# Encoder layer with two attention branches: first modulation chunk on VectorE, rotary angles split, first cosine products on VectorE

## The reference

```python
mod = silu(c) @ w_ada + b_ada;  shift, scale, gate = split(mod, 3)
h = rms_norm(x, norm_pre) * (1 + scale) + shift
proj = h @ w_in          # qa ka va za qd kd vd zd gm, 11264 columns
qa, ka, qd, kd = rope(..., positions)   # [x1*cos - x2*sin, x2*cos + x1*sin]
ya = merge(dilated windows of qa, ka, va) * silu(za);  pa = ya @ w_proj_a
yd = rms_norm(differential_attention(qd, kd, vd)) * silu(zd);  pb = yd @ w_proj_b
ga, gb = split(sigmoid(gm));  y = (ga * pa + gb * pb) @ w_out
out = x + gate * rms_norm(y, norm_post)
```

## Time and profile before

| | |
|---|---|
| median of 3 runs | 847.47 us (846.45 to 848.08) |
| the profiled execution | 846.08 us |
| its span | 844.2 us |
| TensorE busy (PE) | 798.7 us, 95% of the span |
| VectorE (DVE), ScalarE (ACT), GpSimd (POOL) | 54%, 43%, 55% |
| granted clock of TensorE, mean | 0.983 |
| the chain that ended last | PE 71%, DVE 13%, issue 7%, ACT 4%, DMA 2% |

### The profile page before, as it was taken

The page is one execution under the profiler, slowest core; times in us unless marked ns, Lnnn a source line. Parts: engine busy times, 40 slices in busy tenths (PEclk is TensorE's granted clock), DMA queues, the critical chain, the costliest instruction groups (busy, mean ns, idle before and its releaser), DMA issues.

```text
span 844.2 us, 12690 instructions
## 1 busy us (share of the span) xinstructions
PE 798.7 (95%) x4614; PEld 672.0 (80%) x4614; DVE 454.4 (54%) x708; ACT 359.9 (43%) x777; POOL 466.4 (55%) x620
## 2 busy tenths in 40 slices
PE   5887999998999999999989998998999999999997
PEld 5666898886788888889768778877877778888897
DVE  3765363656736354334597588579657653103532
ACT  4543644443335444423435444454466442323310
POOL 4455642555627566377476486679357367647200
PEclk9999899999899999999999999999999999999999
DMA  9933323257333434144522243143112113324431
GB/s 318 326 124 99 101 76 114 76 172 244 97 113 88 136 91 126 50 126 121 147 75 76 82 120 102 51 139 101 50 51 75 51 53 122 101 75 135 165 100 50
DMA packets 87075, 95.38 MB, mean 113 GB/s; under 512 B 9405, under 2 KB 78310, under 8 KB 87014
## 3 DMA queue, kind: packets, MB, share of 16 engines
q1 hardware_dynamic: 86944, 94.56, 36.4%
q10 hardware_dynamic: 70, 0.02, 0.0%
HBM read 78.53 MB, written 5.54 MB: 100 GB/s over the span
## 4 chain that ended last, share of the span: by engine, by line
PE 71%; DVE 13%; issue 7%; ACT 4%; DMA 2%; SPq 1%; POOL 1%; DVEq 0%; POOLq 0%; ACTq 0%
PE proj L1695 49%; PE proj L1829 4%; PE sums L1620 3%; PE score L1570 3%; PE turned L1588 2%; PE proj L1753 2%; DVE dstat L1319 2%; PE score L1536 2%; ACT probs L1025 2%; PE sums L1622 2%; DVE dstat L1335 1%; DVE at_lo L1342 1%; DVE q_lo L1275 1%; PE score L1558 1%; ACT junk L1057 1%
## 5 line engine op out<-in xcount | busy, mean ns | idle before, releaser
L779 POOL TENSOR_TENSOR w_lo<-raw,w_hi 128x256 fp32r<-128x256 f32 x376 | 297.5, 822 | 212.9 <-ACT w_hi L901 212.8
L1695 PE MATMUL proj<-h_hi,w_hi 128*128 128x512 f32 x560 | 230.1, 411 | 0.0
L1695 PE MATMUL proj<-h_hi,w_lo 128*128 128x512 f32 x560 | 220.4, 394 | 0.0
L1695 PE MATMUL proj<-h_lo,w_hi 128*128 128x512 f32 x560 | 218.9, 391 | 0.0
L1695 PEld LDWEIGHTS proj<-h_hi,w_hi 128*128 128x128 f32 x560 | 105.7, 189 | 29.8 <-issue 8.9
L1695 PEld LDWEIGHTS proj<-h_hi,w_lo 128*128 128x128 f32 x560 | 105.5, 188 | 23.7
L1695 PEld LDWEIGHTS proj<-h_lo,w_hi 128*128 128x128 f32 x560 | 106.1, 189 | 19.7 <-issue 0.5
L901 ACT ACTIVATE w_hi<-raw 128x1024 fp32r<-128x1024 f32 x96 | 100.2, 1053 | 11.8 <-PE proj L1695 7.8
L809 POOL TENSOR_TENSOR rope_x<-rope_x,cos_t 128x512 f32<-128x512 f32 x36 | 56.7, 1574 | 75.4 <-DMA rope_s<-rope_x 75.4
L1342 DVE TENSOR_TENSOR at_lo<-turned,at_hi 128x512 fp32r<-128x512 f32 x64 | 44.0, 688 | 61.3 <-ACT at_hi L1043 60.7
L1025 ACT ACTIVATE probs<-score,dstat 128x512 f32<-128x512 f32 x64 | 43.4, 684 | 59.3 <-DVE dstat L1319 59.3
(11 more groups left out here) (286 smaller groups left out, 1563.0 us busy)
## 6 DMA issues: line engine op xcount, KB each, us to landing
raw<-in_w_in SPq DMA_DIRECT2D x85, 512.0 KB, 3.6
rope_s<-rope_x SPq DMA_DIRECT2D x144, 64.0 KB, 2.3
ada<-in_w_ada SPq DMA_DIRECT2D x24, 256.0 KB, 7.1
zd<-in_w_ada SPq DMA_DIRECT2D x8, 512.0 KB, 6.3
raw<-in_w_proj_b SPq DMA_DIRECT2D x8, 512.0 KB, 3.4
raw<-in_w_out SPq DMA_DIRECT2D x8, 512.0 KB, 4.2
rows_in<-window_rows SPq DMA_DIRECT2D x4, 792.0 KB, 4.8
window_rows<-rows_out SPq DMA_DIRECT2D x4, 528.0 KB, 3.7
```

Of the source, the lines that this page charges most:

```text
L779: nc.gpsimd.tensor_tensor(lo[:, k, :], raw_place(n)[:, k, :], hi.bitcast(F32)[:, k, :], ALU.subtract).then_inc(w_lo_done, 1)
L1695: ins = mm(dst, left, right, start=k == 0 and n == 0, stop=k == nk - 1 and n == 2, skip_group_check=tile.b == 2)
```

## The change

Five things are changed.
- VectorE sums all eight pieces of chunk 0; `ada_piece` and its three groups of eight matmuls are gone. The two copies of turned x stand behind piece 5.
- The angle work is cut in two: four instructions (position to the number of turns) ahead of modulate(0), seven (`angle_rest`) behind the last sum of chunk 2, with one sum of chunk 3 behind them, and then modulate(2).
- The sums of a chunk begin ahead of the modulate of the chunk before (one sum), and three instead of one stand ahead of the first h_rest.
- ScalarE's three Sin stand behind `cut_hi` of half 4 instead of behind half 2; SP stores the tables behind the last piece of chunk 3 and half 5.
- The cosine products of the first four tiles are made by VectorE from the PSUM banks into a tensor of their own (`first_cos_x`), ahead of tick 8. GpSimd no longer makes them. TensorE's `bank_free` waits for them too. In all ticks VectorE evacuates the v banks of stage 0 ahead of the rotary work instead of behind it.

```diff
--- before.py
+++ after.py
@@ -178,9 +178,7 @@
     mix_turn_at = by_tick(range(NT), lambda tt: free_turn(mix_tick[tt] + 4))
     vt_at = by_tick([t for t in tiles if t.kind == "vt"], lambda t: free_turn(t.last + (1 if t.j else 2)))
     G_TICK = 36
-    N_CH, PE_ADA = 4, (2, 5, 7)
-    DVE_ADA = [[kk for kk in range(KT) if ch or kk not in PE_ADA] for ch in range(N_CH)]
-    ADA_SUMS = [sum(len(p) for p in DVE_ADA[:ch + 1]) for ch in range(N_CH)]
+    N_CH = 4
     gate_row_at = by_tick(range(2), lambda i: G_TICK + KT + 1 + i)
     ya_split_tick = T0[10] + 4
     LAST_TICK = max(END, max(s.pv for s in steps) + 5)
@@ -342,6 +340,10 @@
         first_raw = sb("first_raw", [P, RAW, 4, BW], on=second)
         h_f = sb("h_f", [P, 2, S], on=second)
         second.close()
+        third = ExitStack()
+        sb("ahead_of_at", [P, 2, D], on=third)
+        first_cos_x = sb("first_cos_x", [P, 4, S], on=third)
+        third.close()
 
 
         def stage_tensors(parity, on):
@@ -455,6 +457,7 @@
         angle_done = sem("angle_done")
         lam_dots = sem("lam_dots")
         silu_done = sem("silu_done")
+        first_cos_done = sem("first_cos_done")
         xt_dve = sem("xt_dve")
         x_norm_done = sem("x_norm_done")
         ab_done = sem("ab_done")
@@ -580,6 +583,11 @@
             n = rope_no[tile.u]
             return (zd[:, n, :], zd[:, 4 + n, :]) if n < 4 else (rope_x2[:, n % 2, :], rope_s2[:, n % 2, :])
 
+        def cos_place(tile):
+
+            n = rope_no[tile.u]
+            return first_cos_x[:, n, :] if n < 4 else rope_place(tile)[0]
+
         def swapped_wait(engine, tile):
             n = rope_no[tile.u]
             if n < 4:
@@ -632,16 +640,16 @@
             sp.wait_ge(x_turned, KT)
             for kk in range(4):
                 load_ada(3, kk)
+            for kk in range(4, KT):
+                load_ada(3, kk)
+            load_half(5)
             sp.wait_ge(act_sin, 3)
             sp.dma_start(trig_rows.rearrange("q f a n -> (q f) a n"), trig).then_inc(trig_stored, 16)
-            for kk in range(4, KT):
-                load_ada(3, kk)
             sp.wait_ge(trig_stored, 16)
             for i in range(4):
                 for table, a in ((cos_t, 2), (sin_t, i % 2)):
                     sp.dma_start(table[32 * i:32 * i + 32, :].rearrange("f (q n) -> f q n", q=NT),
                                  trig_rows[:, :, a, :].rearrange("q f n -> f q n")).then_inc(trig_loaded, 16)
-            load_half(5)
             for i, v in enumerate((lambda_q1, lambda_k1, lambda_q2, lambda_k2)):
                 sp.dma_start(lam_in[:, i, :], v[0].partition_broadcast(P)).then_inc(small_loaded, 16)
 
@@ -801,10 +809,8 @@
             for half in prep_at(-1)[6:]:
                 cut_lo(half)
             for t in range(8, LAST_TICK + 1):
-                for tile in tiles[2 * (t - 8):2 * (t - 7)] if t < 10 else rope_at(t) if t >= 12 else []:
+                for tile in rope_at(t) if t >= 12 else []:
                     swapped_wait(pool, tile)
-                    if rope_no[tile.u] == 0:
-                        pool.wait_ge(trig_loaded, 128)
                     at = rope_place(tile)[0]
                     nc.gpsimd.tensor_tensor(at, at, cos_t[:], ALU.mult).then_inc(rope_cos_done, 1)
                 for half in prep_at(t):
@@ -940,16 +946,16 @@
             h_round(1)
             h_full(1)
             cut_hi(halves[2])
+            for k in (2, 3):
+                h_round(k)
+                h_full(k)
+            cut_hi(halves[3])
+            cut_hi(halves[4])
             act.wait_ge(angle_done, 1)
             for a, sign in enumerate((-1.0, 1.0)):
                 nc.scalar.activation(trig[:, a, :], angle, ACT.Sin, scale=sign).then_inc(act_sin, 1)
             act.wait_ge(angle_done, 2)
             nc.scalar.activation(trig[:, 2, :], complement, ACT.Sin).then_inc(act_sin, 1)
-            for k in (2, 3):
-                h_round(k)
-                h_full(k)
-            cut_hi(halves[3])
-            cut_hi(halves[4])
             for k in (4, 5):
                 h_round(k)
                 h_full(k)
@@ -1156,16 +1162,17 @@
                 dve.wait_ge(ada_loaded[ch][kk], 16)
                 kept = ada[ch][:, 0, :, :]
                 total = turned[:].rearrange("p (r n) -> p r n", r=2) if ch else kept
-                n = DVE_ADA[ch].index(kk)
-                if n == 0:
+                if kk == 0:
                     if ch == 0:
                         dve.wait_ge(silu_done, 1)
                     elif ch == 1:
                         dve.wait_ge(xt_act, 3)
+                    else:
+                        dve.wait_ge(ada_used, KT * ch)
                     ins = ts_(total, kept, silu_c[:, 1, 0:1], None, ALU.mult)
                 else:
-                    dve.wait_ge(ada_used, ADA_SUMS[ch] - len(DVE_ADA[ch]) + n)
-                    ins = stt(out=kept if kk == DVE_ADA[ch][-1] else total, in0=ada[ch][:, kk, :, :],
+                    dve.wait_ge(ada_used, KT * ch + kk)
+                    ins = stt(out=kept if kk == KT - 1 else total, in0=ada[ch][:, kk, :, :],
                               scalar=silu_c[:, 1, kk:kk + 1], in1=total, op0=ALU.mult, op1=ALU.add)
                 ins.then_inc(ada_used, 1)
 
@@ -1191,6 +1198,9 @@
                 link(ts_(angle, angle, rope_c[:, 0:1], None, ALU.mult))
                 link(ts_(turns, angle, float(1 / (2 * np.pi)), ROUND, ALU.mult, ALU.add))
                 link(ts_(turns, turns, ROUND, None, ALU.subtract))
+
+            def angle_rest():
+
                 for part in TWO_PI:
                     link(stt(out=angle, in0=turns, scalar=-part, in1=angle, op0=ALU.mult, op1=ALU.add))
                 ts_(angle, angle, PI_BELOW, -PI_BELOW, ALU.min, ALU.max).then_inc(angle_done, 1)
@@ -1198,32 +1208,37 @@
                 link(stt(out=complement, in0=angle, scalar=-1.0, in1=angle, op0=ALU.mult, op1=ALU.max))
                 ts_(complement, complement, -1.0, float(np.pi / 2), ALU.mult, ALU.add).then_inc(angle_done, 1)
 
-            for kk in DVE_ADA[0][:-1]:
+            for kk in range(6):
                 sum_ada(0, kk)
             for k in (4, 5):
                 dve.wait_ge(x_turned, k + 1)
                 nc.vector.tensor_copy(xt[:, k, :], turn_place(k)).then_inc(xt_dve, 1)
-            sum_ada(0, DVE_ADA[0][-1])
+            sum_ada(0, 6)
+            sum_ada(0, 7)
             dve.wait_ge(cols_done, 2)
+            angles()
             modulate(0)
-            angles()
-            sum_ada(1, 0)
+            for kk in range(3):
+                sum_ada(1, kk)
             h_rest(0)
-            sum_ada(1, 1)
+            sum_ada(1, 3)
             h_rest(1)
-            for kk in range(2, KT):
+            for kk in range(4, KT):
                 sum_ada(1, kk)
+            sum_ada(2, 0)
             modulate(1)
-            for kk in range(KT):
+            for kk in range(1, KT):
                 sum_ada(2, kk)
+            angle_rest()
+            sum_ada(3, 0)
             modulate(2)
-            sum_ada(3, 0)
             sum_ada(3, 1)
+            sum_ada(3, 2)
             h_rest(4)
-            sum_ada(3, 2)
             sum_ada(3, 3)
+            sum_ada(3, 4)
             h_rest(5)
-            for kk in range(4, KT):
+            for kk in range(5, KT):
                 sum_ada(3, kk)
             modulate(3)
             h_rest(6)
@@ -1248,6 +1263,15 @@
                 link(tt_(lam[:, 4:5], lam[:, 2:3], lam[:, 3:4], ALU.subtract))
                 link(ts_(lam[:, 5:6], lam[:, 4:5], LAMBDA_INIT, -1.0, ALU.add, ALU.mult))
                 link(ts_(cols[:, 41:42], cols[:, 40:41], 1.0 - LAMBDA_INIT, None, ALU.mult))
+
+            def first_cos(tile):
+                n = rope_no[tile.u]
+                dve.wait_ge(proj_done, tile.u + 1)
+                dve.wait_ge(rope_copied, n + 1)
+                if n == 0:
+                    dve.wait_ge(trig_loaded, 128)
+                stt(out=cos_place(tile), in0=proj[:, tile.u % 4, :], scalar=SCALE if tile.kind == "q" else 1.0, in1=cos_t[:],
+                    op0=ALU.mult, op1=ALU.mult).then_inc(first_cos_done, 1)
 
             def rope_turn(tile):
                 n = rope_no[tile.u]
@@ -1261,11 +1285,14 @@
                 n = rope_no[tile.u]
                 at, other = rope_place(tile)
                 dve.wait_ge(rope_sin_done, n + 1)
-                dve.wait_ge(rope_cos_done, n + 1)
+                if n < 4:
+                    dve.wait_ge(first_cos_done, n + 1)
+                else:
+                    dve.wait_ge(rope_cos_done, n - 3)
                 if n:
                     dve.wait_ge(rope_lo_done, n)
                 for dst, view in in_order(rope_o[:], tile):
-                    ins = tt_(dst, view(at), view(other), ALU.add)
+                    ins = tt_(dst, view(cos_place(tile)), view(other), ALU.add)
                 ins.then_inc(rope_done, 1)
 
             def rope_cut(tile):
@@ -1420,6 +1447,9 @@
```

(40 more changed lines are left out.)

## The result

| | before | after |
|---|---|---|
| median, measured together, 4 runs each | 847.78 us (846.45 to 851.1) | 838.46 us (837.12 to 838.84) |
| ratio of the two, 95% interval | | 0.9885 (0.9865 to 0.9904) |
| the profiled execution | 846.08 us | 837.12 us |
| its span | 844.2 us | 835.3 us |
| granted clock, mean | 0.983 | 0.979 |

A forecast was written before the change was run, and what follows sets the result against it. TensorE, nearly always busy, was taken to set the pace behind the first attention steps, so gains ahead reach the end. Terms -4.6, -4.4, -3.6, +2.9 gave -9.7: 836.4, or 837.8 us on the median's scale; range 832 to 844.5.

The forecast's parts named there:

- The sum: Whole kernel: opening -4.6, rotary -4.4, clock -3.6, new wait +2.9, in all 9.7 us earlier.
- Chunk 0: Opening: VectorE's sums replace three TensorE groups, first modulate near 19.5 instead of 23.76; gain there 4.2 us.
- Chunks 1 to 3: Opening: modulation(3) at 52.2 instead of 56.77, 4.6 us gained (bounds 3.6 and 5.5); seven angle instructions taken as 5.0 us.
- SP's queue: Tables' store takes 3.7 us (bounds 2 and 8.4); half 6 issued at 54.7, landed at 58.3; slack 0.8 us.
- The rival by SP's queue: Slow store and loads land half 6 at 68, eating the rotary gain; up to 853.5 us; slower had chance 0.07.
- First cosine products and v: Rotary part: VectorE's products cost nothing, last v at 74.5, first scores at 75.5, 9.0 us earlier; TensorE idles 1.2 us.
- The clock: Behind the first scores the upper level stays: scores 1.6 us instead of 3.2, 24 products 5.7 instead of 7.69; -3.6.
- The new wait: Ahead of TensorE's second transpose: 2.9 us, as GpSimd's cuts and the swap of tile 8 come only 7.0 us earlier.
- Where the step failed: Behind the second transpose: TensorE busy without break, nothing found that gives back time from the 9.7 us gained.
- given back: Rival: TensorE drops to the lower clock in the new wait, up to 3.5 us lost, 841.5 to 844.5; chance 0.20.
- a fall of the clock behind 76: Sign of being wrong: the granted clock falls behind 76 us, where 1.00 was forecast behind the first scores.
- More gained: Rival: the shifted 3.4 us wait up to 208.3 isn't followed by the slow clock; up to 4.5 us more, 833; chance 0.13.

The follow-up runs named there:

- c0_after: The changed kernel run and profiled again, with nothing altered: 838.77 us, 0.9894 of before.
- e8: The changed kernel with pieces 2, 5 and 7 of chunk 0 given back to TensorE: 840.47 us, 0.991 of before.
- e10: The changed kernel with the seven angle instructions ahead of modulate(1) and SP's swaps ahead of the loads of halves in every tick: 825.5 us, 0.9752 of before.
- e11: The kernel before with SP's swaps ahead of the loads of halves in every tick, nothing else: 842.57 us, 0.9942 of before.
- e9: The kernel before with only chunk 0 changed, VectorE summing all eight pieces: 841.76 us, 0.993 of before.
- e1: The changed kernel with the rotary part as before (cosine products by GpSimd, v behind the rotary work), so the opening alone: 841.74 us, 0.9939 of before.
- e5: The changed kernel with SP issuing the swap of tile 8 ahead of the loads of halves it stood behind: 833.15 us, 0.9832 of before.
- e2: The kernel before with only the rotary part changed (first cosine products by VectorE, v evacuated ahead): 845.65 us, 0.9979 of before.

## Why the prediction was right, point by point

The sum had -9.7 on the profile's scale and the profiles gave -9.0; the median came out 0.7 us above 837.8. The mechanism held up to the second transpose. The terms were off by more than the sum, and that their deviations cancelled in part was luck.

- **Chunk 0.** Modulation(0) ended, and with it modulate began, at 18.75 instead of 19.5, projection at 20.37 instead of 21.1. Over all profiles the gain at modulation(0) was 3.2 us, with 4.2 forecast.
- **Chunks 1 to 3.** -6.7 instead of -4.6 in the first profile, beyond the bound of 5.5; -5.1 in c0_after, within it; mean -5.9. The working took the lower clock in the first products as given; in the first profile it rose at 25 (clock 0.99 in 25 to 30), and modulation(1) came at 29.76, not 32.5. The seven angle instructions took 4.62 us, with 5.0 taken.
- **SP's queue.** The store landed in 1.9 us, with 3.7 taken and 8.4 as bound:

```profile
42.04 0.35 SPq L647 DMA_DIRECT2D trig_rows<-mstat  x1
43.95 0.34 SPq L651 DMA_DIRECT2D cos_t<-trig_rows  x1
...
49.56 1.53 SPq L621 DMA_DIRECT2D raw<-in_w_in  x3
```

The loads of halves 6 to 8 went out from 49.56 instead of 54.7, and ScalarE waited 0.91 for half 6, ahead of where it mattered:

```profile
55.58 1.06 ACT L907 ACTIVATE v<-raw 128x1024 fp32r<-128x1024 f32 x1 [0.91 <-DMA raw<-in_w_in]
58.11 1.09 ACT L972 ACTIVATE zd<-proj 128x512 f32<-128x512 f32 x2 [1.47 <-PE proj L1780]
```

ScalarE's copies waited 1.47 us for TensorE, not for the half: covered, with 1.47 of slack instead of 0.8. The rival by SP's queue was never near.
- **First cosine products and v.** From the swap's landing to the start of the last v 9.0 us were forecast; 63.44 to 72.46 is 9.0. VectorE's four products, in pairs of 1.29 us, lay in its waits and cost nothing. TensorE's wait is 1.17 us, with 1.2 forecast:

```profile
58.80 1.29 DVE L1273 SCALAR_TENSOR_TENSOR first_cos_x<-proj,cos_t 128x512 f32<-128x512 f32 x2 [2.94 <-ACT zd L972]
...
63.44 0.69 DVE L1282 TENSOR_TENSOR zd<-zd,sin_t 128x512 f32<-128x512 f32 x1 [0.62 <-DMA zd<-zd]
...
72.46 0.68 DVE L1310 TENSOR_TENSOR v<-score,v 128x512 fp32r<-128x512 f32 x1
```

- **The clock.** 1.00 from 73 to 88, as forecast. From the first scores to the second transpose before took 15.51 us, after 14.75, of which 2.39 are the wait: 3.15 us gained by the clock, with 3.6 forecast.
- **The new wait.** 2.39 us ahead of the second transpose, 2.9 forecast, by the path forecast: cuts of halves 8 and 9, SP's queue, the swap of tile 8. GpSimd started its cuts at 76.16 (2.1 ahead of the 78.3 forecast, as everything ahead was).
- **Where the step failed.** "From there TensorE is busy without break and I find nothing that gives time back." The new wait was followed by 0.50, which gave back 1.7 us by 95 and is the rival "given back" in its mechanism, to which the forecast gave 0.20. It came in the four profiles with a wait of 2.3 to 2.5 us there (e8's is the fourth) and in none with a shorter one. The prediction had a fall of the clock behind 76 as a sign of being wrong, and the fall came at 90. What it held against this rival, that the shorter waits of TensorE "leave no mark that I found in the clock", isn't so in the trace of before itself. TensorE's wait up to 517.05, and the clock a us behind it:

```profile
517.05 0.66 PE L1588 MATMUL turned<-ident,probs 128*128 128x128 f32 x4 [2.49 <-DVE za L1421]
```

```profile
518.00:521.00 3.00, 3.00 (x17) 2.63 (x14) 2.17 (x4) 1.37 (x4) 2.18 (x11) 0.58 1.00 334
```

A further 1.2 went into VectorE's stretch up to 421 and the lower clock behind it. That the end is still near the forecast is due to the opening, which had gained 1.3 to 2 us more.
- **More gained** didn't come with the change: the wait up to 208 is still there (3.21 us up to 198.01, a clock of 0.69 in 195 to 206, where it was 0.50 for nine us), and from the fifth to the twentieth at_lo only 0.4 us came on top. e10 and e11 show that 5 us and more lay there, but for another edit.

What stays open: why the parts don't add (e9, e1 and e8 above), and which wait the lower clock follows where the waits are short. The Trainium skill, page TensorE: Matmul & The Clock Gate, section "HAM oscillation — how this bites in real kernels", tells that idle gaps let the clock fall back. The runs agree in kind (no gap and no fall in e5's 74 to 94). The section at the end counts which waits were followed by a fall.

## What to carry to other kernels

A queue that issues in order makes a small urgent transfer as late as the big one ahead of it, and a load that waits for its buffer shows as one row whose time is far above its issues (17.75 us for four): put the urgent transfer ahead of it. Ask of each gain which front comes next and on which queue its transfer stands; here the change's own new wait and the clock behind it cost 4 to 6 us, and the same cure elsewhere gave 5 to 7 us that had mostly lain in the kernel before. There it wasn't SP that stood, but the landing that was late, behind the load. One profile is good to 1 to 3 us for a step of a kernel like this, so take the steps' sizes from several and let the medians decide.

## What was not expected of the hardware

A short wait of TensorE, 2.3 to 2.5 us between stretches of full work, was followed by some three us at 0.50 in four profiles (after, c0_after, e2, e8), one to two us behind its end. Ahead of the first scores, waits of 1.9 us were followed by it in both profiles that had them, waits of 1.2 us in one of eight. But the length of a wait alone doesn't decide. Over all waits of TensorE of 1 us and more from 73 us on, in all fourteen profiles, the lower clock came within five us behind

| wait of TensorE | waits | followed by the lower clock |
|---|---|---|
| 1.0 to 1.5 us | 42 | 1 |
| 1.52 to 1.75 us | 16 | 8 |
| 1.89 to 2.49 us, for other work than `za` | 11 | 10 |
| 2.48 to 2.50 us, the two for `za` between 497 and 588 us | 26 | 14 |
| 2.6 us and more | 23 | 23 |

The fourth row is the odd one: the waits are as long as each other, and in each of the twelve profiles that have both, exactly one of the two was followed by some three us at 0.50, in before and after the first, in c0_after the second. What decides between them no run here shows.

The level in the opening differs between profiles of one kernel: 1.05 against 1.86 us for the same eight matmuls. VectorE's small instructions lose the larger part of their speed beside GpSimd: 0.23 became 0.65 us at 128x128, where 128x512 went from 0.69 to 1.21 (the sine products). The store of the tables landed in 1.9 us, where the same store behind a full queue had taken 8.4.
